# Turned scores of two latent units in four row groups, units of neighbouring head pairs alternating

## The chip, the cores and the metric

One core of a Trainium2 chip runs one program, and the metric is its device time in microseconds, the median of several executions. In what follows PE is TensorE, DVE is VectorE, ACT is ScalarE, POOL is GpSimd and SP is the engine that issues the loads.

## The reference, cut to what matters

The program is a network of ten phases over 512 tokens of width 1024 in fp32: feed-forward layers, a windowed-attention mixer, a state-space mixer, and at the end two layers of a second kind (mixer "mix2", then a feed-forward layer). Only the second kind of mixer is changed. It has a grouped attention of 8 heads and a latent attention of 8 heads; each latent head has 64 plain ("nope") and 32 rotated ("rope", here: turned) score dimensions, and all heads share one turned key:

```python
qb = (rmsnorm(cq, q_a_norm_g) @ w_q_up).reshape(b, s, MLA_HEADS, MLA_QK_DIM)
q_nope, q_rope = qb[..., :MLA_NOPE_DIM], qb[..., MLA_NOPE_DIM:]     # 64 and 32 wide
q_rope = apply_axial_rope(q_rope, cos_b, sin_b)
k_nope, vb = kvb[..., :MLA_NOPE_DIM], kvb[..., MLA_NOPE_DIM:]
k_rope = apply_axial_rope(kr, cos_b, sin_b)                          # one for all heads
qb = jnp.concatenate([q_nope, q_rope], axis=-1)[:, :, :, None, :]
kb = jnp.concatenate([k_nope, k_rope], axis=-1)
yb = blocked_attention(qb, kb, vb, 1.0 / math.sqrt(MLA_QK_DIM))      # softmax(q k^T) v
gates = jax.nn.sigmoid(gl + b_gate)
merged = g_a * (ya @ w_branch_a) + g_b * (yb @ w_branch_b)
return merged @ w_o
```

The score of a latent head is so a sum of two products, one over 64 rows and one over 32 rows.

## The kernel before, in words

**Units.** Attention is worked off in units. A unit is 128 queries (block n of 4) of a pair of heads (the two "sides"), against all 512 keys. A mix2 layer has 32 units: 16 grouped ones (4 head pairs of 4 blocks, `grouped_units`, L1607) and then 16 latent ones (`latent_units`, L1615), pair j = 0 to 3 outside, block n inside. Side 0 of a pair lies in partitions 0 to 63, side 1 in 64 to 127. The turned parts are packed by four heads: head 2j + side lies in the 32 partitions of quarter (2j + side) % 4 of `b_qr[:, j // 2]`, and `b_kr` holds the shared turned key four times, once in each quarter.

**One step of PE** (`attend_pe`, L744). Step s issues in this order, waits included, since every engine works its queue in order:
- the scores of unit s into `scores[g % 2]`, g being the running number of the unit: for a grouped unit one product per side over 64 rows (the pair of sides runs in two row groups); for a latent unit that pair of 64-row products and then a pair of 32-row products on top (L757 to L760). It waits for the exponentials of unit g - 2 (`probs_ready`, L755), which free the buffer;
- the transposes of unit s - 3 (BEHIND = 3, L773), side 0 into bank 5 and side 1 into bank 6, when POOL has scaled it (`probs_scaled`) and the banks have been copied out (`copied_a`, `copied_b`);
- the product with the values of unit s - 4 (L786, "attend"), into bank 4 or 7 (HEADS), which the head pairs use in turn. The first unit of a head pair waits until the pair before the last has been read out (`head_split`, L782).

**The other engines.** DVE (`attend_dve`) takes the row maximum of unit s (L800), scales it (L806, L809), inverts the sums of unit s - 1 (L816), copies side 1 of the turned probabilities of unit s - 3 (L822), and at the end of a head pair forms its low part (L827) one step after ACT formed the high part (L858). ACT (`attend_act`) copies side 0 of unit s - 3 (L838), then does the exponentials of unit s (L850, two sides, each with a read of its sum), then the high part of a head pair that has ended. POOL (`attend_pool`) multiplies the probabilities by the inverted sums (L866). Nothing is loaded that this stretch waits for.

**The end of the attention.** `fill` lists work put ahead of a step: in mix2 two "gate" projections (24 products each, L289 to L291) at steps 34 and 35, each with a wait for all exponentials and for the split of all head pairs but the last (L749, L750). They write the next accumulator bank, tile number % 5 (ACCS), counted through the program. The attention of the first mix2 layer ends at tile 336, that of the second at tile 464, so the first gate writes bank 1 in the first layer and bank 4, which is also one of HEADS, in the second. After the last attend PE waits for the last head pair to be split and begins the branch products (L1798 to L1800).

The step in the code that the change replaces:

```python
many = len(u["q"][0])
for part in range(many):
    for side in range(2):
        mm = pe.matmul(scores[g % 2][:, side, 0:u["keys"]], u["q"][side][part], u["k"][side][part],
                       start=part == 0, stop=part == many - 1)
```

Of the kernel before, what the change touches and what calls it, by code (L numbers as in the profile page):

```python
# [126 lines left out]
def build(nc, t, stop=99):  # L127
    with ExitStack() as ctx:
# [615 lines left out]
        def attend_pe(pe, c, units, turned, fill):  # L744

            n = len(units)
            for s in range(n + BEHIND + 1):
                if s in fill:
                    pe.wait_ge(probs_ready, c.units + n)  # L749
                    pe.wait_ge(head_split, c.heads + n // 4 - 1)  # L750
                    fill[s]()
                if s < n:
                    u, g = units[s], c.units + s
                    if g >= 2:
                        pe.wait_ge(probs_ready, g - 1)  # L755
                    many = len(u["q"][0])
                    for part in range(many):  # L757
                        for side in range(2):
                            mm = pe.matmul(scores[g % 2][:, side, 0:u["keys"]], u["q"][side][part], u["k"][side][part],  # L759
                                           start=part == 0, stop=part == many - 1)  # L760
                    for side in range(2):
                        for at, mask in u["masks"]:
                            mm = pe.matmul(scores[g % 2][:, side, at:at + P], e_ident[:], e_mask[:, mask, :], start=False,
                                           stop=True, skip_group_check=True)
                    mm.then_inc(scores_ready, 1)
                if 0 <= s - BEHIND < n:
                    u, g = units[s - BEHIND], c.units + s - BEHIND
                    pe.wait_ge(probs_scaled, g + 1)
                    for side, (done, free) in enumerate(((turned_a, copied_a), (turned_b, copied_b))):
                        if g:  # L770
                            pe.wait_ge(free, g)
                        for j in range(u["keys"] // P):
                            mm = pe.transpose(bank[TURNED + side][:, j * P:(j + 1) * P],  # L773
                                              pbuf[:, g % 4, side, j * P:(j + 1) * P], ident[:])
                        mm.then_inc(done, 1)
                if 0 <= s - BEHIND - 1 < n:
                    u, g = units[s - BEHIND - 1], c.units + s - BEHIND - 1
                    pe.wait_ge(copied_a, g + 1)
                    pe.wait_ge(copied_b, g + 1)
                    hd = c.heads + (s - BEHIND - 1) // 4  # L780
                    if (s - BEHIND - 1) % 4 == 0 and hd >= 2:
                        pe.wait_ge(head_split, hd - 1)  # L782
# [8 lines left out]
        def attend_dve(dve, ch, c, units, turned):  # L791
            n = len(units)
            for s in range(n + BEHIND + 3):
# [29 lines left out]
                e = s - BEHIND - 2  # L823
                if 0 <= e < n and e % 4 == 3:
                    u, hd = units[e], c.heads + e // 4
                    dve.wait_ge(head_rounded, hd + 1)
                    dve.tensor_tensor(u["lo"], bank[HEADS[hd % 2]][:], u["hi"].bitcast(F32), ALU.subtract)\  # L827
                       .then_inc(head_split, 1)

        def attend_act(act, c, units, turned):  # L830
            n = len(units)
            for s in range(n + BEHIND + 2):
# [21 lines left out]
                e = s - BEHIND - 1  # L854
                if 0 <= e < n and e % 4 == 3:
                    u, g, hd = units[e], c.units + e, c.heads + e // 4
                    act.wait_ge(attended, g + 1)
                    act.activation(u["hi"], bank[HEADS[hd % 2]][:], ACT.Copy).then_inc(head_rounded, 1)  # L858
# [17 lines left out]
        def even_units():  # L876
            units = []
            for j, pair in enumerate(EVEN_PAIRS):
                keys = pair[0] // 3 // 2
                for n in range(NB):  # L880
                    lo, hi = max(n - 1, 0), min(n + 1, NB - 1)
                    halves = (slice(0, HD), slice(HD, P))
                    units.append(dict(
                        q=[[e_qk[half, 2 + j, n * P:(n + 1) * P]] for half in halves],
                        k=[[e_qk[half, keys, lo * P:(hi + 1) * P]] for half in halves],
                        keys=(hi - lo + 1) * P, scale=HD ** -0.5, col=None, n=n, nsink=e_nsink[:, j, :],
# [28 lines left out]
        def even_pe(pe, c, e):  # L915
# [36 lines left out]

            def pooled_part():
                pe.wait_ge(pool_split, 2)
                pe.wait_ge(w_rest, B + OPEN)
# [651 lines left out]
        def grouped_units():  # L1607
            halves = (slice(0, HD), slice(HD, P))
            return [dict(q=[[b_qk[half, j, n * P:(n + 1) * P]] for half in halves], k=[[b_qk[half, 4, :]] for half in halves],
                         keys=S, col=8 * j + 2 * n, n=n, nsink=None, masks=[],  # L1610
# [4 lines left out]
        def latent_units():  # L1615
            halves = (slice(0, HD), slice(HD, P))
            quarters = [slice(32 * i, 32 * i + 32) for i in range(4)]
            return [dict(q=[[b_qn[halves[side], j, n * P:(n + 1) * P],
                             b_qr[quarters[(2 * j + side) % 4], j // 2, n * P:(n + 1) * P]] for side in range(2)],
                         k=[[b_kn[halves[side], j, :], b_kr[quarters[(2 * j + side) % 4], :]] for side in range(2)],  # L1620
                         keys=S, scale=QK ** -0.5, col=None, n=n, nsink=None, masks=[],
                         v=[[b_vb[:, j, m * P + side * HD:m * P + (side + 1) * HD] for m in range(4)] for side in range(2)],
                         hi=yb_hi[:, j, :], lo=yb_lo[:, j, :])
                    for j in range(4) for n in range(4)]

# [53 lines left out]
        def mix2_pe(pe, c, e):  # L1679
# [99 lines left out]
            units = grouped_units() + latent_units()  # L1779

            def gate():
                project(pe, k, k.tiles, [xs_of(xh, xl, KD)])
                k.tiles += 1
            attend_pe(pe, k, units, mix2_turned, {len(units) + BEHIND - 1: gate, len(units) + BEHIND: gate})
            for m in range(KD):
                if m:
                    gate()
                    gate()
                else:
                    pe.wait_ge(head_split, c.heads + len(units) // 4)  # L1790
# [552 lines left out]
```

## Time and profile before

| | |
|---|---|
| median of 3 runs | 3642.07 us (3642.05 to 3642.74) |
| the profiled execution's own time | 3638.86 us |
| its span, first to last instruction | 3637.1 us |
| granted TensorE clock, mean | 0.991 |
| PE busy | 3552.4 us (98%) |
| DVE, ACT, POOL busy | 1432.1, 1342.4, 1899.8 us |
| HBM read | 296.46 MB, 82 GB/s over the span |

The profile is one execution. The span lies within the execution's own time; the difference is what surrounds the program. A busy share is an average over all ten phases. Whether an edit to one phase counts is read from the waits and the order of time in that phase. A matmul in fp32 shows as two records (two passes over the same columns), and two matmuls in different row groups show as records that overlap.

### The profile page before, as it was taken

To read this page: it belongs to the slowest core of one execution; us is meant where nothing else is said; L and a number is where in the kernel's file an instruction comes from. 1 tells how busy PE (TensorE), PEld (TensorE's weight loads), DVE (VectorE), ACT (ScalarE), POOL (GpSimd) and SP (SyncE) were. 2 spreads that over 40 slices of the span, in tenths; PEclk is the share of its full clock that TensorE was granted. 3 is DMA by queue.
4 is the path that set the end of the run, shared out by engine and by line. 5 is a ranking of instruction groups with operands and counts; after the bars stand their busy time and mean duration, and the time that the engine had idled before them with its cause. 6 is when DMAs were issued, how large, how long until landed. Compare 5 with 4: busy or idle time off the path is not lost.

```text
span 3637.1 us, 45438 instructions
## 1 busy us (share of the span) xinstructions
PE 3552.4 (98%) x18086; PEld 2847.0 (78%) x18086; DVE 1432.1 (39%) x2315; ACT 1342.4 (37%) x2172; POOL 1899.8 (52%) x2364
## 2 busy tenths in 40 slices
PE   8999999999999999999999999999999999999998
PEld 7888868888888888548888875778888866878887
DVE  4221765221532158775321355325111564234022
ACT  4232354232422235564332336334232344334231
POOL 6555546555555557525655455545555454546452
PEclk9999999999999999999999999999999999999999
DMA  3333302333232323102333320222333210323332
GB/s 129 96 92 96 104 23 94 96 95 96 92 99 93 94 94 99 38 14 88 99 95 95 108 71 1 64 87 88 99 93 99 91 47 12 93 81 96 96 94 74
DMA packets 87715, 301.50 MB, mean 83 GB/s; under 512 B 9936, under 2 KB 14544, under 8 KB 87120
## 3 DMA queue, kind: packets, MB, share of 16 engines
q1 hardware_dynamic: 85392, 296.50, 26.2%
q8 instruction: 144, 2.36, 0.3%
q10 hardware_dynamic: 2112, 2.10, 0.2%
q14 instruction: 67, 0.55, 0.0%
HBM read 296.46 MB, written 2.10 MB: 82 GB/s over the span
## 4 chain that ended last, share of the span: by engine, by line
PE 91%; DVE 7%; ACT 1%; issue 0%; DMA 0%; SPq 0%; DVEq 0%; ACTq 0%
PE bank L289 25%; PE bank L291 25%; PE bank L290 24%; PE scores L759 3%; PE bank L786 2%; PE bank L773 2%; DVE sqsum L453 1%; DVE xl L443 1%; DVE x L418 1%; DVE tmp L411 1%; PE bank L1798 1%; PE bank L1800 1%; PE bank L1799 1%; PE bank L505 1%; PE bank L506 1%; PE bank L1238 1%
## 5 line engine op out<-in xcount | busy, mean ns | idle before, releaser
L283 POOL TENSOR_TENSOR w_lo<-w_raw,w_hi 128x256 fp32r<-128x256 f32 x2214 | 1681.9, 793 | 1451.6 <-ACT w_hi L271 1451.0
L271 ACT ACTIVATE w_hi<-w_raw 128x1024 fp32r<-128x1024 f32 (+2 forms) x567 | 586.3, 1037 | 1235.4 <-DMA w_raw<-in_ffn_up 374.0
L289 PE MATMUL bank<-xh,w_hi 128*128 128x512 f32 x2544 | 998.1, 392 | 1.2 <-DVE o_g L1449 1.2
L291 PE MATMUL bank<-xh,w_lo 128*128 128x512 f32 x2544 | 990.1, 389 | 0.0
L290 PE MATMUL bank<-xl,w_hi 128*128 128x512 f32 x2544 | 990.0, 389 | 0.0
L289 PEld LDWEIGHTS bank<-xh,w_hi 128*128 128x128 f32 x2544 | 478.4, 188 | 103.7 <-issue 3.1
L290 PEld LDWEIGHTS bank<-xl,w_hi 128*128 128x128 f32 x2544 | 478.5, 188 | 100.0 <-issue 2.4
L291 PEld LDWEIGHTS bank<-xh,w_lo 128*128 128x128 f32 x2544 | 478.4, 188 | 100.0
L289 PE MATMUL bank<-hh,w_hi 128*128 128x512 f32 (+1 forms) x1336 | 501.9, 376 | 0.0
L290 PE MATMUL bank<-hl,w_hi 128*128 128x512 f32 (+1 forms) x1336 | 500.8, 375 | 0.0
L291 PE MATMUL bank<-hh,w_lo 128*128 128x512 f32 (+1 forms) x1336 | 500.8, 375 | 0.0
L290 PEld LDWEIGHTS bank<-hl,w_hi 128*128 128x128 f32 x1336 | 251.2, 188 | 50.0
L289 PEld LDWEIGHTS bank<-hh,w_hi 128*128 128x128 f32 x1336 | 251.1, 188 | 50.0
L291 PEld LDWEIGHTS bank<-hh,w_lo 128*128 128x128 f32 x1336 | 251.1, 188 | 49.9
L866 POOL TENSOR_TENSOR work<-work,red 128x1024 f32<-128x1024 f32 (+2 forms) x88 | 151.3, 1720 | 149.9 <-DVE red L816 149.9
L672 DVE TENSOR_TENSOR work<-bank,sqsum 128x512 f32<-128x512 f32 x88 | 60.7, 690 | 360.9 <-PE bank L291 360.9
L740 DVE COPY y<-bank 128x512 f32<-128x512 f32 x49 | 33.9, 691 | 425.5 <-PE bank L291 425.5
L505 PE MATMUL bank<-xh,w_hi 128*128 128x256 f32 x480 | 124.6, 289 | 19.1 <-ACT xh L475 19.1
L800 DVE TENSOR_REDUCE red<-scores 128x2 f32<-128x1024 f32 (+2 forms) x88 | 98.1, 1115 | 95.0 <-PE scores L759 90.3
L659 ACT ACTIVATE hh<-work 128x512 fp32r<-128x512 f32 x88 | 55.7, 633 | 183.8 <-DVE work L676 183.8
L506 PE MATMUL bank<-xh,w_lo 128*128 128x256 f32 x480 | 122.6, 285 | 0.0
L669 DVE TENSOR_TENSOR work<-bank,sqsum 128x512 f32<-128x512 f32 x88 | 60.8, 691 | 156.5 <-PE bank L291 156.4
(361 smaller groups left out, 4116.5 us busy)
## 6 DMA issues: line engine op xcount, KB each, us to landing
w_raw<-in_ffn_up SPq DMA_DIRECT2D x176, 512.0 KB, 3.5
w_raw<-in_ffn_down SPq DMA_DIRECT2D x64, 512.0 KB, 3.5
w_raw<-in_b_ffn_up SPq DMA_DIRECT2D x64, 512.0 KB, 3.5
w_raw<-in_b_ffn_down SPq DMA_DIRECT2D x64, 512.0 KB, 3.5
w_raw<-in_b_gates SPq DMA_DIRECT2D x48, 512.0 KB, 3.5
w_raw<-in_od_in SPq DMA_DIRECT2D x33, 512.0 KB, 3.3
w_raw<-in_ffn_down SPq DMA_DIRECT2D x32, 384.0 KB, 3.1
w_raw<-in_b_in SPq DMA_DIRECT2D x24, 512.0 KB, 3.3
```

The lines of the kernel that those rows point to most:

```text
L271: act.activation(w_hi[:, g % RING, 0:widths[g]], w_raw[:, g % RING, 0:widths[g]], ACT.Copy)\
L283: ins = pool.tensor_tensor(w_lo[:, slot, part], w_raw[:, slot, part], w_hi[:, slot, part].bitcast(F32), ALU.subtract)
L289: pe.matmul(out, wh, hi, start=first, stop=False)
L290: pe.matmul(out, wh, lo, start=False, stop=False)
L291: return pe.matmul(out, wl, hi, start=False, stop=last)
L505: pe.matmul(out, w_hi[:, slot, k * P:(k + 1) * P], xh[:, k, half(h)], start=k == 0, stop=False)
L506: pe.matmul(out, w_lo[:, slot, k * P:(k + 1) * P], xh[:, k, half(h)], start=False, stop=False)
L759: mm = pe.matmul(scores[g % 2][:, side, 0:u["keys"]], u["q"][side][part], u["k"][side][part], start=part == 0, stop=part == many - 1)
L773: mm = pe.transpose(bank[TURNED + side][:, j * P:(j + 1) * P], pbuf[:, g % 4, side, j * P:(j + 1) * P], ident[:])
L786: mm = pe.matmul(bank[HEADS[hd % 2]][side * HD:(side + 1) * HD, u["n"] * P:(u["n"] + 1) * P], u["v"][side][j], turned[g % 2][:, side, j * ...
L800: ch.link(dve.reduce_max(r[:, 0:2], scores[g % 2][:, :, 0:u["keys"]], mybir.AxisListType.X))
L866: pool.tensor_tensor(p, p, red[:, g % 4, 8:10].unsqueeze(2).broadcast_to([P, 2, u["keys"]]), ALU.mult)\
```

## The change

It does the following.

- Latent units of neighbouring head pairs alternate: (pair 0, block 0), (pair 1, block 0), (pair 0, block 1), and so on, then pairs 2 and 3. The order of all other work on a unit stays.
- The 64-row product of each latent unit stays where it was. The 32-row products of two following units, four matmuls, are issued together ("joint") in the step of the first of them, after that step's transposes and ahead of its attend. They lie in the four quarters of the partitions and write the four banks of both score buffers. The first unit's two add to its 64-row product, the second unit's two open its sum, and its 64-row product is added in the next step.
- Since the joint products write both score buffers, they wait for the exponentials of unit g - 1, not g - 2. The first unit's `scores_ready` is given after the second of the four.
- The running head number comes from the unit (`head`), and so do the ends of the heads (`n == 3`), since two head pairs are now open at once.
- The wait for `head_split` moves out of `attend_pe` into the fills. In mix2 it is taken only where a gate writes bank 4 or 7; where the first gate does (`late`), it is issued at step 35 instead of 34, and the second one behind the last attend.

```diff
--- before.py
+++ after.py
@@ -747,22 +747,20 @@
             for s in range(n + BEHIND + 1):
                 if s in fill:
                     pe.wait_ge(probs_ready, c.units + n)
-                    pe.wait_ge(head_split, c.heads + n // 4 - 1)
                     fill[s]()
                 if s < n:
                     u, g = units[s], c.units + s
                     if g >= 2:
                         pe.wait_ge(probs_ready, g - 1)
-                    many = len(u["q"][0])
-                    for part in range(many):
-                        for side in range(2):
-                            mm = pe.matmul(scores[g % 2][:, side, 0:u["keys"]], u["q"][side][part], u["k"][side][part],
-                                           start=part == 0, stop=part == many - 1)
+                    for side in range(2):
+                        mm = pe.matmul(scores[g % 2][:, side, 0:u["keys"]], u["q"][side], u["k"][side],
+                                       start=u["opens"], stop=u["closes"], skip_group_check=True)
                     for side in range(2):
                         for at, mask in u["masks"]:
                             mm = pe.matmul(scores[g % 2][:, side, at:at + P], e_ident[:], e_mask[:, mask, :], start=False,
                                            stop=True, skip_group_check=True)
-                    mm.then_inc(scores_ready, 1)
+                    if not u["joint"]:
+                        mm.then_inc(scores_ready, 1)
                 if 0 <= s - BEHIND < n:
                     u, g = units[s - BEHIND], c.units + s - BEHIND
                     pe.wait_ge(probs_scaled, g + 1)
@@ -773,12 +771,20 @@
                             mm = pe.transpose(bank[TURNED + side][:, j * P:(j + 1) * P],
                                               pbuf[:, g % 4, side, j * P:(j + 1) * P], ident[:])
                         mm.then_inc(done, 1)
+                if s < n and units[s]["joint"]:
+                    u, g = units[s], c.units + s
+                    pe.wait_ge(probs_ready, g)
+                    for q, (query, key) in enumerate(u["joint"]):
+                        mm = pe.matmul(scores[(g + q // 2) % 2][:, q % 2, 0:u["keys"]], query, key, start=q >= 2, stop=q < 2,
+                                       skip_group_check=True)
+                        if q == 1:
+                            mm.then_inc(scores_ready, 1)
                 if 0 <= s - BEHIND - 1 < n:
                     u, g = units[s - BEHIND - 1], c.units + s - BEHIND - 1
                     pe.wait_ge(copied_a, g + 1)
                     pe.wait_ge(copied_b, g + 1)
-                    hd = c.heads + (s - BEHIND - 1) // 4
-                    if (s - BEHIND - 1) % 4 == 0 and hd >= 2:
+                    hd = c.heads + u["head"]
+                    if u["n"] == 0 and hd >= 2:
                         pe.wait_ge(head_split, hd - 1)
                     many = u["keys"] // P
                     for j in range(many):
@@ -821,8 +827,8 @@
                         dve.wait_ge(attended, g - 1)
                     dve.tensor_copy(turned[g % 2][:, 1, 0:u["keys"]], bank[TURNED + 1][:, 0:u["keys"]]).then_inc(copied_b, 1)
                 e = s - BEHIND - 2
-                if 0 <= e < n and e % 4 == 3:
-                    u, hd = units[e], c.heads + e // 4
+                if 0 <= e < n and units[e]["n"] == 3:
+                    u, hd = units[e], c.heads + units[e]["head"]
                     dve.wait_ge(head_rounded, hd + 1)
                     dve.tensor_tensor(u["lo"], bank[HEADS[hd % 2]][:], u["hi"].bitcast(F32), ALU.subtract)\
                        .then_inc(head_split, 1)
@@ -852,8 +858,8 @@
                                              accum_out=r[:, 4 + side:5 + side])
                     ins.then_inc(probs_ready, 1)
                 e = s - BEHIND - 1
-                if 0 <= e < n and e % 4 == 3:
-                    u, g, hd = units[e], c.units + e, c.heads + e // 4
+                if 0 <= e < n and units[e]["n"] == 3:
+                    u, g, hd = units[e], c.units + e, c.heads + units[e]["head"]
                     act.wait_ge(attended, g + 1)
                     act.activation(u["hi"], bank[HEADS[hd % 2]][:], ACT.Copy).then_inc(head_rounded, 1)
 
@@ -881,8 +887,9 @@
                     lo, hi = max(n - 1, 0), min(n + 1, NB - 1)
                     halves = (slice(0, HD), slice(HD, P))
                     units.append(dict(
-                        q=[[e_qk[half, 2 + j, n * P:(n + 1) * P]] for half in halves],
-                        k=[[e_qk[half, keys, lo * P:(hi + 1) * P]] for half in halves],
+                        q=[e_qk[half, 2 + j, n * P:(n + 1) * P] for half in halves],
+                        k=[e_qk[half, keys, lo * P:(hi + 1) * P] for half in halves],
+                        opens=True, closes=True, joint=None, head=j,
                         keys=(hi - lo + 1) * P, scale=HD ** -0.5, col=None, n=n, nsink=e_nsink[:, j, :],
                         masks=[((m - lo) * P, mask) for m, mask in ((n - 1, 0), (n + 1, 1)) if lo <= m <= hi],
                         v=[[e_v[:, keys, m * P + half.start:m * P + half.stop] for m in range(lo, hi + 1)] for half in halves],
@@ -951,6 +958,7 @@
                             mm.then_inc(blocks_done, 1)
 
             def pooled_part():
+                pe.wait_ge(head_split, c.heads + len(units) // 4 - 1)
                 pe.wait_ge(pool_split, 2)
                 pe.wait_ge(w_rest, B + OPEN)
                 columns_of((0,))
@@ -1606,7 +1614,8 @@
 
         def grouped_units():
             halves = (slice(0, HD), slice(HD, P))
-            return [dict(q=[[b_qk[half, j, n * P:(n + 1) * P]] for half in halves], k=[[b_qk[half, 4, :]] for half in halves],
+            return [dict(q=[b_qk[half, j, n * P:(n + 1) * P] for half in halves], k=[b_qk[half, 4, :] for half in halves],
+                         opens=True, closes=True, joint=None, head=j,
                          keys=S, col=8 * j + 2 * n, n=n, nsink=None, masks=[],
                          v=[[b_va[:, m * P + half.start:m * P + half.stop] for m in range(4)] for half in halves],
                          hi=ya_hi[:, j, :], lo=ya_lo[:, j, :])
@@ -1614,14 +1623,14 @@
 
         def latent_units():
             halves = (slice(0, HD), slice(HD, P))
-            quarters = [slice(32 * i, 32 * i + 32) for i in range(4)]
-            return [dict(q=[[b_qn[halves[side], j, n * P:(n + 1) * P],
-                             b_qr[quarters[(2 * j + side) % 4], j // 2, n * P:(n + 1) * P]] for side in range(2)],
-                         k=[[b_kn[halves[side], j, :], b_kr[quarters[(2 * j + side) % 4], :]] for side in range(2)],
+            rows = [slice(32 * i, 32 * i + 32) for i in range(4)]
+            return [dict(q=[b_qn[half, j, n * P:(n + 1) * P] for half in halves], k=[b_kn[half, j, :] for half in halves],
+                         opens=j % 2 == 0, closes=j % 2 == 1, head=4 + j,
+                         joint=[(b_qr[r, j // 2, n * P:(n + 1) * P], b_kr[r, :]) for r in rows] if j % 2 == 0 else None,
                          keys=S, scale=QK ** -0.5, col=None, n=n, nsink=None, masks=[],
                          v=[[b_vb[:, j, m * P + side * HD:m * P + (side + 1) * HD] for m in range(4)] for side in range(2)],
                          hi=yb_hi[:, j, :], lo=yb_lo[:, j, :])
-                    for j in range(4) for n in range(4)]
+                    for first in (0, 2) for n in range(4) for j in (first, first + 1)]
 
         mix2_turned = [tmp, b_turned]
 
@@ -1778,15 +1787,19 @@
             k.tiles = c.tiles + len(TILES2)
             units = grouped_units() + latent_units()
 
+            late = k.tiles % ACCS in HEADS
+
             def gate():
+                if k.tiles % ACCS in HEADS:
+                    pe.wait_ge(head_split, c.heads + len(units) // 4 - 1)
                 project(pe, k, k.tiles, [xs_of(xh, xl, KD)])
                 k.tiles += 1
-            attend_pe(pe, k, units, mix2_turned, {len(units) + BEHIND - 1: gate, len(units) + BEHIND: gate})
+            attend_pe(pe, k, units, mix2_turned, {len(units) + BEHIND: gate} if late else
+                      {len(units) + BEHIND - 1: gate, len(units) + BEHIND: gate})
             for m in range(KD):
-                if m:
+                for _ in range(2 if m else 1 if late else 0):
                     gate()
-                    gate()
-                else:
+                if m == 0:
                     pe.wait_ge(head_split, c.heads + len(units) // 4)
                 slot = take_block(pe, k)
                 for q, (hi, lo) in enumerate(((ya_hi, ya_lo), (yb_hi, yb_lo))):
```

## Rows read from the trace of the kernel before

**Rows 1.** The page: span, busy time, granted clock by slice, chain that ended last.

```profile
span 3637.1 us, 45438 instructions
...
PE 3552.4 (98%) x18086; PEld 2847.0 (78%) x18086; DVE 1432.1 (39%) x2315; ACT 1342.4 (37%) x2172; POOL 1899.8 (52%) x2364
...
PEclk9999999999999999999999999999999999999999
...
PE 91%; DVE 7%; ACT 1%; issue 0%; DMA 0%; SPq 0%; DVEq 0%; ACTq 0%
```

**Rows 2.** Windows, the two latent stretches: length, busy by engine, granted clock, DMA share.

```profile
2224.72:2291.36 66.64, 66.64 (x515) 36.98 (x513) 35.17 (x69) 34.85 (x85) 30.31 (x17) 1.00 0.00 1
3004.53:3071.17 66.64, 66.64 (x515) 36.98 (x513) 35.16 (x69) 34.86 (x85) 30.32 (x17) 1.00 0.01 1
```

**Rows 3.** Timeline, PE, one latent step: start, length, engine, line, operation, count.

```profile
2253.88 1.13 PE L759 MATMUL scores<-b_kn,b_qn 64*128 64x512 f32 x4
2254.93 1.13 PE L759 MATMUL scores<-b_kr,b_qr 32*128 32x512 f32 x4
2255.99 1.09 PE L773 MATMUL bank<-ident,work 128*128 128x128 f32 x8
2257.02 1.09 PE L786 MATMUL bank<-b_turned,b_vb 128*64 128x128 f32 x16
2258.04 1.13 PE L759 MATMUL scores<-b_kn,b_qn 64*128 64x512 f32 x4
```

**Rows 4.** Timeline, DVE, ACT and POOL, the same latent step.

```profile
2256.11 1.23 DVE L800 TENSOR_REDUCE red<-scores 128x2 f32<-128x1024 f32 x1 [2.08 <-PE scores L759]
2257.37 0.17 DVE L809 TENSOR_SCALAR red<-red 128x2 f32<-128x2 f32 x1
2257.45 0.16 DVE L816 RECIPROCAL red<-red 128x2 f32<-128x2 f32 x1
2257.52 0.67 DVE L822 COPY tmp<-bank 128x512 f32<-128x512 f32 x1
...
2256.69 0.60 ACT L838 ACTIVATE tmp<-bank 128x512 f32<-128x512 f32 x1 [1.83 <-PE bank L773]
2257.57 0.69 ACT L850 ACTIVATE work<-scores,red 128x512 f32<-128x512 f32 x1 [0.29 <-DVE red L809]
...
2258.82 0.20 ACT L850 ACTIVATION_READ_ACCUMULATOR work<-scores,red 128x1 f32 x1
2258.91 0.59 ACT L858 ACTIVATE yb_hi<-bank 128x512 fp32r<-128x512 f32 x1
...
2257.68 1.89 POOL L866 TENSOR_TENSOR work<-work,red 128x1024 f32<-128x1024 f32 x1 [2.27 <-DVE red L816]
```

**Rows 5.** Timeline, PE, narrow windows: single passes of the pairs and the first transposes.

```profile
2254.41 0.60 PE L759 MATMUL scores<-b_kn,b_qn 64*128 64x512 f32 x2
2254.93 0.70 PE L759 MATMUL scores<-b_kr,b_qr 32*128 32x512 f32 x2
...
2177.07 1.02 PE L759 MATMUL scores<-b_qk 64*128 64x512 f32 x4
...
2177.49 1.02 PE L759 MATMUL scores<-b_qk 64*128 64x512 f32 x4
...
2255.99 0.44 PE L773 MATMUL bank<-ident,work 128*128 128x128 f32 x2
```

**Rows 6.** Timeline, the last grouped exponential and the first latent transposes.

```profile
2225.68 0.20 ACT L850 ACTIVATION_READ_ACCUMULATOR work<-scores,red,stat 128x1 f32 x1
...
2226.84 1.09 PE L773 MATMUL bank<-ident,work 128*128 128x128 f32 x8
```

**Rows 7.** Timeline, the last attend of the second layer and what follows it.

```profile
3088.54 1.09 PE L786 MATMUL bank<-b_turned,b_vb 128*64 128x128 f32 x16
...
3090.31 0.69 DVE L827 TENSOR_TENSOR yb_lo<-bank,yb_hi 128x512 fp32r<-128x512 f32 x1 [7.67 <-ACT yb_hi L858]
...
3091.06 0.51 PE L1798 MATMUL bank<-ya_hi,w_hi 128*128 128x512 f32 x1 [1.42 <-DVE yb_lo L827]
```

## The prediction

> **What bounds the kernel now.** I read the page first. PE is busy for 98% of the span, the chain that ended last lies on it for 91%, and the granted clock is full in all slices [rows 1]. That says PE, but an average over ten phases can hide a phase with another limit, so I read the two stretches that the change touches, the sixteen latent units of each mix2 layer, by windows. In both, PE is busy for 66.64 us of 66.64, at clock 1.00, while DVE, ACT and POOL stand at 35, 35 and 30 us and the DMA share is zero [rows 2]. A unit costs 66.64 / 16 = 4.165 us. The timeline of PE within one unit shows what that is: a pair of 64-row products, a pair of 32-row products, the transposes, the attend, and the next unit's scores follow with no gap [rows 3]. From start to start these stages take 1.06 (2253.88 to 2254.93), 1.06, 1.02 and 1.02 us. The 32-row pair fills half as many rows as the 64-row pair and takes as long. So what counts here is the number of stages that PE works through, as long as the others keep up.
>
> **The change, part by part.** About 0.2% (7 us) is what a measurement of this kernel can tell from no change.
>
> *The 32-row products.* Per two units the change removes two 32-row pair stages, 2 x 1.06 = 2.12 us, and adds one stage of four. The trace has no such stage, so its price is bounded. From below: the pair's own 1.06 us, if four run side by side as two do. From above: 2.12 us, if the two pairs follow each other. Serial work of all four, 4.24 us, is further off, and nothing in the trace has 32-row products of different row groups one by one. To choose I take the stage apart. In the layer's first units, where pair follows pair with no change of shape between them, a pass starts 0.43 us after the one before (2177.07 to 2177.49) [rows 5]. Two passes are 0.86, so a pair stage of 1.06 carries 0.20 us beyond them, once as it begins and once as it ends: its first pass takes 0.53 us (2253.88 to 2254.41), its second 0.52 to the next shape [rows 3, 5]. The transposes do nearly the same with one load exposed at their start instead of two: two of them end at 0.44 us and all eight at 1.09, so one is (1.09 - 0.44) / 6 = 0.108, eight are 0.87, and the stage of 1.02 carries 0.15 to 0.16. An exposed weight load of 128 columns is therefore worth about 0.05 us, and four loads instead of two add 0.10. I take 1.16 us for the stage of four: 0.86 of passes, 0.20 of loads, 0.10 of change of shape. It is nearest to the 32-row pair in every respect but the number of loads.
>
> The Trainium skill, page "TensorE: Matmul & The Clock Gate", section on packing small matmuls, has a rule that speaks for less: four 32-row products side by side were measured there at 3.07 times one after another, not four times. With a pair's 1.06 us for one product, that would be 4 x 1.06 / 3.07 = 1.38 us, an estimate by that page, and the sum below would be 11.8 us of gain. No row here shows a stage of four.
>
> Gain: 2.12 - 1.16 = 0.96 us per two units, eight times in a layer, in two layers: 16 x 0.96 = 15.4 us. A layer's two units go from 8.33 to 7.37 us.
>
> *The new wait.* The joint stage waits for the exponentials of unit g - 1. Behind it in PE's queue are the attend of unit g - 4, the next unit's products and everything after; DVE's row maximum waits for it. I put the chain against PE's order, with t the start of the joint stage of an even unit e. PE: joint to 1.16, attend to 2.18, 64-row pair of e + 1 to 3.24, transposes to 4.26, attend to 5.29, 64-row pair to 6.35, transposes to 7.37, next joint. Chain, by the spacings of one unit [rows 4]: DVE starts 0.12 us after the stage's end (2255.99 to 2256.11), ACT's exponentials 1.46 us after that (2257.57), and they take 1.45 us (to 2259.02). For e that is 1.28, 2.74, 4.19. Scores of e + 1 are ready at 3.24; DVE, after the inverse and the copy of 0.67 us, is free at 3.36 and starts; its results would allow the exponentials at 4.82, ACT has copied side 0 (0.60) by 4.79, so they run from 4.82 to 6.27. The next joint is due at 7.37: a slack of 1.1 us, so the wait costs nothing. Where head pairs end, ACT's high part (0.59) and DVE's low part (0.69, rows 7) fall into the chain in different steps, each taking 0.6 or 0.7 of that slack; 0.4 us are left. If this cover went, each 0.1 us of lateness would cost 1.6 us in all.
>
> *Other waits of the new order.* POOL's scaling of e - 1 starts about 2.85 and ends at 4.74 (1.89 us [rows 4]); its transposes come at 6.35. The copy of side 1 of e - 3 ends at 3.36; the transposes that overwrite its bank reach side 1 at about 3.75. This is the tightest place, 0.4 us. The first joint stage comes where the transposes start at 2226.84 today, and the last grouped exponentials end at 2225.88 [rows 6]: no stall. The first unit of a head pair now follows two units after the end of the pair whose bank it takes; its low part is done at about 4.05, its attend due at 4.26. Price if missed: the few tenths by which it is late, some six times in all.
>
> *The end of the attention.* First layer: bank 1, the gates stay where they are; the `head_split` wait that leaves the fill was long satisfied. Second layer: bank 4, so one gate moves behind the last attend. Today PE stands for 1.42 us between the last attend and the first branch product, for the high and low part of the last head pair [rows 7]. After the change the last but one unit ends the pair in bank 4, so the same 1.4 us come ahead of the first gate, and the second gate covers the ones that are there today. Zero in sum. No other queue has a step moved past it: SP and POOL have the same orders, and the loads of the next blocks wait for the same gates in the same order. The even mixer issues what it issued; its `head_split` wait moves within the same fill. Zero.
>
> *Sum.* The profiled execution took 3638.86 us (span 3637.1); less 15.4 that is 3623.5. The median of the runs is 3.2 us above it, so 3642.07 - 15.4 = 3626.7 us.
>
> **The rivals.**
> *The loads of the second passes are not hidden either.* Then both passes of a stage of four pay four loads, 2 x (0.43 + 0.20) + 0.10 = 1.36 us; gain 0.76 x 16 = 12.2, time 3629.9 us. Against it: pair after pair runs at 0.43 us a pass, loads hidden [rows 5]; for it: no row has four loads behind one pass. The page of the Trainium skill named above would land here.
> *The four run only two by two,* by a conflict over four score banks at once or for lack of look-ahead past the first pair. The stage is 2.02 to 2.12 us, the change doesn't do what it says, gain 0 to 1.6 us, time 3641 to 3642 us. For it: the trace never has more than two row groups at work. Against it: the attend's two sides and both pairs start together and show no cost of company.
> *The new wait becomes the bound (slower).* If DVE or ACT took the units strictly one after another, a pair would last twice the chain from scores to exponentials, 2 x 3.03, plus joint and 64-row stage, 1.16 + 1.06, plus one copy ahead of each exponential, 2 x 0.6: 9.5 us against 8.33, so 16 x 1.15 = 18 us slower, 3660 us. It decides once the chain of two units passes 8.33 us; my count gives 6.3 and 1.1 of slack to PE's own 7.37. A chain between 7.4 and 8.3 gives back part of the gain, 3627 to 3641.
>
> **How the numbers follow.** The stage of four at 1.06 to 1.2 us with no stall: 0.66 (3625 to 3627.5). Loads exposed: 0.17. Chain late in part: 0.06. Two by two: 0.07. Slower: 0.04. The range holds the first two and small stalls of up to 0.1 us per two units: low end at the 1.06 bound, 17.0 us of gain, less a microsecond of spread between runs, 3624; high end 3629.9 plus 1.6 and spread, 3632. Faster by over 0.2% are the first two and most of the third, 0.88; within it the two-by-two case and the rest of the third, 0.08; slower 0.04.
>
> **What would show it.** The latent windows should last about 59 us instead of 66.64 with PE busy throughout; the stage of 32-row products should appear once per two units, eight records, with a length from its start to the attend's of 1.16 us; the wait of PE for ACT's exponentials ahead of it should be absent; the stall of 1.4 us in the second layer should stand ahead of the first gate and no longer ahead of L1798. A stage of four over 1.3 us speaks for the first rival, about 2.1 for the second, and PE idle ahead of the joint stage for the third. Unchanged latent windows make the prediction wrong.

## The result, and the profile after

The changed kernel takes 3622.09 us (median of 5, 3619.07 to 3625.31) against 3642.05 for the kernel before (3634.18 to 3642.74): ratio 0.995, interval 0.9938 to 0.9962, 20.0 us less. Five more runs on another occasion, in turns with fifteen of the kernel before, gave 3622.04 against 3638.09: 16.1 us less, ratio 0.9957, interval 0.9944 to 0.9969. The profiled execution took 3619.07 us, its span is 3617.2.

The page after, the lines that answer to [rows 1]:

```profile
span 3617.2 us, 45434 instructions
...
PE 3535.4 (98%) x18086; PEld 2844.0 (79%) x18086; DVE 1433.0 (40%) x2315; ACT 1340.5 (37%) x2172; POOL 1895.6 (52%) x2364
...
PEclk9999999999999999999999999999999999999999
```

The page shows next to nothing: PE was the bound and is the bound (the chain that ended last lies on it for 92%, before for 91%), and no matmul has gone (x18086 in both). The windows of the two latent stretches, cut so that they hold the same 515 records of PE as in [rows 2], show the gain (length, then busy time of PE, its loads, DVE, ACT, POOL, then granted clock, DMA share, GB/s):

```profile
2222.45:2280.77 58.32, 58.32 (x515) 34.73 (x513) 34.92 (x69) 33.87 (x85) 30.34 (x17) 1.00 0.01 1
2992.49:3050.81 58.32, 58.32 (x515) 34.73 (x513) 34.92 (x69) 33.87 (x85) 30.34 (x17) 1.00 0.01 1
```

The same 515 records take 58.32 us instead of 66.64, PE still without a gap. The timeline of PE, beside [rows 3]:

```profile
2237.02 1.13 PE L756 MATMUL scores<-b_kn,b_qn 64*128 64x512 f32 x4
2238.08 1.09 PE L771 MATMUL bank<-ident,work 128*128 128x128 f32 x8
2239.10 1.14 PE L778 MATMUL scores<-b_kr,b_qr 32*128 32x512 f32 x8
2240.17 1.09 PE L792 MATMUL bank<-tmp,b_vb 128*64 128x128 f32 x16
```

Eight records, the four products, lie in one stage of 1.07 us (2239.10 to 2240.17), where four records took 1.06. A window on the beginning of such a stage, one joint stage earlier, shows how: all eight loads start within 0.13 us (the row spans 0.31, one load 0.18), so they lie beside each other, and the first passes of all four products start together (four records of 0.69 span 0.71).

```profile
2231.81 0.31 PEld L778 LDWEIGHTS scores<-b_kr,b_qr 32*128 32x128 f32 x8 [0.17 <-issue]
...
2231.82 0.71 PE L778 MATMUL scores<-b_kr,b_qr 32*128 32x512 f32 x4
```

The chain through ACT, beside [rows 4]. The second unit's exponentials end at 2237.80 + 0.20 = 2238.00, the joint stage begins at 2239.10: 1.10 us of slack.

```profile
2234.45 0.69 ACT L856 ACTIVATE work<-scores,red 128x512 f32<-128x512 f32 x1 [2.37 <-DVE red L815]
...
2236.55 0.69 ACT L856 ACTIVATE work<-scores,red 128x512 f32<-128x512 f32 x1 [0.16 <-DVE red L815]
...
2237.80 0.20 ACT L856 ACTIVATION_READ_ACCUMULATOR work<-scores,red 128x1 f32 x1
```

This stage is the roomiest kind. Of the eight joint stages of a layer three have 1.10 us of slack, the first 0.93, one 0.89 and three only 0.61 or 0.62, the same in both layers. The small ones stand where head pairs end: ahead of the joint stage at 2246.39, for one, ACT stood idle for 0.66 us until DVE, which had formed a low part before, had the row maximum. No joint stage came late.

The end of the second layer, beside [rows 7]. The stall stands ahead of the first gate (L289), and the branch product follows the second gate at once:

```profile
3055.89 1.09 PE L792 MATMUL bank<-tmp,b_vb 128*64 128x128 f32 x16
3057.03 0.60 ACT L864 ACTIVATE yb_hi<-bank 128x512 fp32r<-128x512 f32 x1 [0.87 <-PE bank L792]
3057.66 0.69 DVE L833 TENSOR_TENSOR yb_lo<-bank,yb_hi 128x512 fp32r<-128x512 f32 x1 [0.97 <-ACT yb_hi L864]
...
3058.45 0.47 PE L289 MATMUL bank<-xh,w_hi 128*128 128x512 f32 x1 [1.47 <-issue]
...
3070.45 0.39 PE L291 MATMUL bank<-xh,w_lo 128*128 128x512 f32 x1
3070.68 0.40 PE L1811 MATMUL bank<-ya_hi,w_hi 128*128 128x512 f32 x1
```

The profile puts this wait down to "issue". That it is the wait for the split is not shown by a releaser; it is read from its place, right behind yb_lo, and from the code.

### The profile page after: what moved, and what is told of

It is laid out like the page before. It is cut to its first block, busy times and chain, and to the rows that moved or that the text cites. A ratio compares the mean times of both kernels' runs of the same rounds, so it can differ in the third digit from the quotient of the medians.

```text
span 3617.2 us, 45434 instructions
## 1 busy us (share of the span) xinstructions
PE 3535.4 (98%) x18086; PEld 2844.0 (79%) x18086; DVE 1433.0 (40%) x2315; ACT 1340.5 (37%) x2172; POOL 1895.6 (52%) x2364
## 4 chain that ended last, share of the span: by engine, by line
PE 92%; DVE 6%; ACT 1%; issue 0%; DMA 0%; SPq 0%; DVEq 0%; ACTq 0%
PE bank L289 25%; PE bank L290 25%; PE bank L291 25%; PE scores L756 2%; PE bank L792 2%; PE bank L771 2%; DVE sqsum L453 1%; DVE xl L443 1%; DVE x L418 1%; DVE tmp L411 1%; PE bank L1811 1%; PE bank L1813 1%; PE bank L1812 1%; PE bank L505 1%; PE bank L506 1%; PE bank L513 1%
## 5 line engine op out<-in xcount | busy, mean ns | idle before, releaser
L289 PE MATMUL bank<-xh,w_hi 128*128 128x512 f32 x2544 | 998.1, 392 | 2.7 <-issue 1.5
L289 PEld LDWEIGHTS bank<-xh,w_hi 128*128 128x128 f32 x2544 | 478.7, 188 | 105.4 <-issue 4.6
L289 PE MATMUL bank<-hh,w_hi 128*128 128x512 f32 (+1 forms) x1336 | 501.9, 376 | 0.0
L289 PEld LDWEIGHTS bank<-hh,w_hi 128*128 128x128 f32 x1336 | 251.1, 188 | 50.2
```

Of the source, the lines that this page charges most:

```text
L289: pe.matmul(out, wh, hi, start=first, stop=False)
```

## The experiments

Theory: the gain is the stage saved, 8 x (2.12 - 1.07) = 8.4 us in each layer, and nothing else; the new wait and the moved gate cost nothing. Rivals: the order gives or costs something of its own; ACT's total work decides and not the place of the wait. One table for all runs, worked out from their timelines: where the first latent product starts in the first layer; the stretch from there to the transposes behind the last 64-row pair; to the first branch product; PE's idle time in the stretch and behind it (each pair of figures is first and second layer). The four kernels with pieces and count_groups were run once each (3621.62, 3626.18, 3624.85, 3630.20 and 3626.27 us, in the order act_pieces8, early_pieces8, act_pieces16, early_pieces16, count_groups); ten runs of the changed kernel lie between 3618.7 and 3626.0, so single times cannot tell them apart by a few us, and their traces are what counts.

| kernel | starts at | stretch | to branch | idle in | idle behind |
|---|---|---|---|---|---|
| before | 2224.72 | 64.58, 64.58 | 86.50, 86.53 | 0, 0 | 1.42, 1.42 |
| changed | 2222.45 | 56.23, 56.23 | 78.12, 78.19 | 0, 0 | 1.42, 1.47 |
| after_again | 2220.61 | 56.23, 56.23 | 78.17, 78.20 | 0, 0 | 1.42, 1.47 |
| alternate_only | 2226.45 | 64.58, 64.58 | 86.47, 86.55 | 0, 0 | 1.42, 1.47 |
| count_groups | 2228.21 | 56.15, 56.15 | 78.09, 78.12 | 0, 0 | 1.42, 1.47 |
| joint_early | 2225.85 | 56.37, 56.38 | 78.31, 78.35 | 0.07, 0.08 | 1.42, 1.47 |
| gates_after | 2229.09 | 56.23, 56.23 | 76.38, 76.92 | 0, 0 | 0, 0.48 |
| act_pieces8 | 2223.96 | 56.23, 56.23 | 78.27, 78.31 | 0, 0 | 1.48, 1.52 |
| early_pieces8 | 2226.82 | 56.38, 56.39 | 78.28, 78.36 | 0.08, 0.08 | 1.42, 1.47 |
| act_pieces16 | 2223.33 | 56.29, 56.29 | 79.33, 79.68 | 0, 0 | 2.44, 2.75 |
| early_pieces16 | 2224.99 | 59.44, 59.44 | 82.36, 82.69 | 2.72, 2.72 | 2.34, 2.66 |

**The changed kernel once more** (no edit).

> The changed kernel once more, in turns with the kernel before on one chip. In the two profiles on hand the latent stretches account for 16.7 us (16 times 2 x 1.06 - 1.07), and some 3 us of the 19.9 us between the spans arose in the state-space mixer, where the granted clock differed (0.77 before, 0.96 after, 1530 to 1545 us). Theory: only the 16.7 us belong to the change. It expects a difference of the medians of 15.5 to 18 us, ratio 0.9954. Rival: the change also moves what comes before and after the latent stretches, difference 19 to 21 us, ratio 0.9945.

Measured: 16.1 us, as the theory has it, and the stretches as in the first trace of the changed kernel. The two stretches give 8.35 us each. The interval of this comparison, 11 to 20 us, would still allow the lower part of the rival's 19 to 21. Two things speak against the rival. All 30 runs of the kernel before have a median of 3639.1 us, the ten of the changed kernel 3622.1, which is 17.0 apart. And in the traces the span without the two parts from the first latent product to the first branch product is 3464.0 us in the kernel before, while over the ten other traces it goes from 3460.5 to 3469.3: the rest of the kernel before takes no longer than that of the others.

What lies ahead of the latent stretches is the same program but for one satisfied wait, and yet the first latent product starts anywhere from 2220.6 to 2229.1 us. A part of it can be placed by the granted clock of the state-space mixer (columns as above, the clock being third from the end), here for the kernel before and the changed one:

```profile
1530.00:1545.00 15.00, 15.00 (x74) 5.45 (x72) 6.65 (x9) 8.16 (x18) 3.86 (x4) 0.77 0.00 1
```

```profile
1530.00:1545.00 15.00, 15.00 (x87) 5.79 (x86) 8.96 (x13) 9.37 (x20) 4.34 (x4) 0.96 0.00 1
```

PE is busy throughout in both, and does 74 instructions at clock 0.77 and 87 at 0.96. In this pair of profiles the changed kernel comes out 2.8 us ahead between 1518 and 1560 us. In another pair it goes the other way: gates_after has 0.93 from 1600 to 1720 us where the changed kernel has 0.97, and loses 3 us there.

**The order alone.** Each latent unit issues its own 32-row pair, and the joint block is gone; units still alternate, gates as in the changed kernel.

```diff
+                    for side, (query, key) in enumerate(u["own"]):
+                        mm = pe.matmul(scores[g % 2][:, side, 0:u["keys"]], query, key, start=False, stop=True,
+                                       skip_group_check=True)
...
-                    if not u["joint"]:
-                        mm.then_inc(scores_ready, 1)
+                    mm.then_inc(scores_ready, 1)
...
-                if s < n and units[s]["joint"]:
...
```

> The units of neighbouring head pairs alternate and the gates stand as in the changed kernel, but each latent unit issues its own pair of 32-row products right behind its 64-row pair, as before. Theory (all of the gain is the stage saved): time as before, within 1.5 us, latent unit 4.165 us. Rival (the order itself gives or costs something through head_split and the moved gate): a difference from before of 2 us or more.

Measured 3639.19 against 3638.09, ratio 1.0003 (0.9994 to 1.0013), stretches of 64.58 us. The medians alone would leave room for up to 4.7 us more. The traces settle it: from the first latent product to the branch products it takes 86.47 and 86.55 us, before 86.50 and 86.53. The order by itself is worth nothing, nor is the moved gate: the stall of 1.47 us only changes its place.

**Row groups counted.**

```diff
-                         joint=[(b_qr[r, j // 2, n * P:(n + 1) * P], b_kr[r, :]) for r in rows] if j % 2 == 0 else None,
+                         joint=[(b_qr[r, j // 2, n * P:(n + 1) * P], b_kr[r, :]) for r in rows[0:n + 1]] if j % 2 == 0 else None,
...
```

> Part of the computation is left out: the joint stage has one 32-row product in block 0, two in block 1, three in block 2, all four in block 3. This measures the stage by the number of row groups. Theory of the prediction (each exposed load costs 0.05 us): 1.01, 1.06, 1.11, 1.16 us, the last of which the changed kernel already contradicts with 1.07. Rival (loads of different row groups run side by side, a row group more costs only the few ns by which it starts later): 1.05, 1.06, 1.065, 1.07 us from the stage's start to the attend's.

The four joint stages of the first two head pairs, each followed by the attend:

```profile
2230.29 1.12 PE L778 MATMUL scores<-b_kr,b_qr 32*128 32x512 f32 x2
2231.34 1.09 PE L792 MATMUL bank<-tmp,b_va 128*64 128x128 f32 x16
...
2237.56 1.13 PE L778 MATMUL scores<-b_kr,b_qr 32*128 32x512 f32 x4
2238.62 1.09 PE L792 MATMUL bank<-tmp,b_va 128*64 128x128 f32 x16
...
2244.83 1.13 PE L778 MATMUL scores<-b_kr,b_qr 32*128 32x512 f32 x6
2245.89 1.09 PE L792 MATMUL bank<-tmp,b_vb 128*64 128x128 f32 x16
...
2252.11 1.14 PE L778 MATMUL scores<-b_kr,b_qr 32*128 32x512 f32 x8
2253.18 1.09 PE L792 MATMUL bank<-tmp,b_vb 128*64 128x128 f32 x16
```

From joint start to attend start: 1.05, 1.06, 1.06, 1.07 us for one, two, three and four row groups. My price of 0.05 us per load is refuted: three row groups more, with six loads more, cost 0.02 us together. This kernel leaves out 24 of the 64 products over 32 rows, so it measures a stage and is no version of the program.

Four products side by side come to 4 x 1.05 / 1.07 = 3.9 times four stages that each hold one product and stand between stages of another shape. No run has four such products directly one after another. By the 0.43 us from pass to pass without a change of shape [rows 5] they would take 8 x 0.43 + 0.20 = 3.6 us, an estimate, and four side by side would be 3.4 times as fast. The Trainium skill, page "TensorE: Matmul & The Clock Gate", section on packing small matmuls, measured 3.07. Both figures of this case lie above it, and the stage of 1.07 us, not the 1.38 that this factor gave, is what decides here. The span model of the Trainium skill in the same section, one product plus some 4 ns for each further one, agrees in kind: 0.02 us for three more.

**The joint stage ahead of the transposes** (the block moved up by one stage).

> The joint stage moves ahead of the step's transposes, so the second unit's scores come one stage of 1.02 us later behind it while the next joint is due after the same 7.29 us. My chain count gives 1.1 us of slack with the joint stage where the change has it; here 0.1 us would be left, and less than none where a head pair ends. Theory: latent stretches 0 to 2 us longer in each layer than in the changed kernel, with PE idle on ACT's exponentials ahead of some joint stages. Rival (the chain has much more slack than I counted): no idle time at all, the same time as the changed kernel.

Measured: 3622.53 us, ratio 0.9955, stretches 0.14 and 0.15 us longer than in the changed kernel, of which 0.07 or 0.08 is idle time.

```profile
2255.91 0.20 ACT L856 ACTIVATION_READ_ACCUMULATOR work<-scores,red 128x1 f32 x1
...
2256.19 1.14 PE L768 MATMUL scores<-b_kr,b_qr 32*128 32x512 f32 x8
```

The exponentials end at 2256.11 and the joint stage begins at 2256.19, so the slack is the 0.1 us that the count gave. It is 0.08 at seven of the eight joint stages of a layer. At the first one the joint stage begins 0.05 us behind the exponentials, the least that these traces show between the two, and there the idle time lies. That the ends of head pairs would break it was wrong. ACT's high part of 0.60 us falls where ACT would otherwise wait for the transposes, 0.78 us in this variant, and no joint stage behind DVE's low part is late either.

**ACT made slower.** Its copy of side 0 is cut into pieces, once with the joint stage where the change has it and once ahead of the transposes.

```diff
-                    act.activation(turned[g % 2][:, 0, 0:u["keys"]], bank[TURNED][:, 0:u["keys"]], ACT.Copy)\
-                       .then_inc(copied_a, 1)
+                    latent = u["nsink"] is None and u["col"] is None
+                    cuts = [round(q * u["keys"] / 8) for q in range(9)] if latent else [0, u["keys"]]
+                    for a, b in zip(cuts, cuts[1:]):
+                        ins = act.activation(turned[g % 2][:, 0, a:b], bank[TURNED][:, a:b], ACT.Copy)
+                    ins.then_inc(copied_a, 1)
```

> ACT's copy of side 0 of a latent unit is made in 8 pieces of 64 columns, which lengthens it from 0.57 us to an estimated 1.6, worked out from the 0.57 us of the whole copy and the 0.09 us after which a read of one column lets the next instruction start. The joint stage stays where the change has it. Theory (a slack of 1.10 us ahead of the joint stage, as the trace of the changed kernel shows): the longer copy takes about 1.0 of it, so no idle time except where a head pair ends, 0 to 1.5 us per layer. Rival (ACT's throughput is already the bound near): 4 us or more per layer.

> The same copy in 8 pieces, and the joint stage ahead of the transposes, where the trace of that variant shows 0.08 us of slack. ACT has the same work as in the run before. Theory (the wait for the exponentials is a chain that the joint stage's place can bring to the path): each joint stage comes 0.4 to 0.8 us late, 3 to 6.5 us more per layer than the changed kernel, with PE idle on ACT's exponentials. Rival (only ACT's total work counts): the same time as the run before.

Within the stretch neither shows more idle time than without the pieces. The next instruction starts only 0.104 us later for each piece (from 2237.30 to 2238.13 for eight). With the joint stage early, the exponentials waited 0.29 us for DVE behind the whole copy (joint_early, copy at 2253.78, exponentials at 2254.67); the longer copy falls into that wait, and they start as long after its beginning as before (2240.18 to 2241.06). So the load was too small to tell the theories apart: inconclusive. With 16 pieces (16 and range(17) in the edit):

> The copy in 8 pieces took 0.83 us from its start to the next instruction, 0.104 us a piece, not the 1.6 I had estimated, so it took too little of the slack to test anything. With 16 pieces of 32 columns it should take 1.66 us, 1.1 us more than the whole copy. The joint stage stays where the change has it. Theory (slack of 1.10 us): it is used up to the last tenth, so PE is idle 0 to 0.15 us per joint stage and up to 0.6 where a head pair ends, 0 to 2.5 us per layer. Rival (ACT's total work decides; per two units it is 2 x (1.45 + 1.66) = 6.2 us of 7.29): no idle time in either of these two runs.

> The same copy in 16 pieces with the joint stage ahead of the transposes. Theory (a chain that the place of the joint stage can bring to the path): in that variant the copy starts when its transposes are done, and the exponentials behind it would begin 0.7 to 0.9 us later than without the pieces, with 0.08 us of slack; so each joint stage comes 0.6 to 0.8 us late, 4.5 to 7 us more per layer than the changed kernel. Rival (ACT's total work decides): no more than the run before.

From the first of sixteen pieces to the next instruction's start it took 1.22 and 1.25 us in the two kernels, not the 1.66 expected. With the joint stage in the change's place PE has no idle time within the stretch. Its joint stages keep 0.47 us of slack or more, but for one in each layer, where a head pair ends: there the load is released by the exponentials, and the stage begins 0.06 us late.

```profile
2269.18 0.31 PEld L778 LDWEIGHTS scores<-b_kr,b_qr 32*128 32x128 f32 x8 [0.23 <-ACT work L859]
```

With the same work on ACT and the joint stage earlier PE does wait for them, as PE's waits of that kernel (2222 to 2290 us; total, times, longest) show:

```profile
PE scores L768 <- ACT work L859: 2.6, 6, 0.5
```

Six joint stages of the layer come late, five by 0.42 us and one by 0.55, and the layer's stretch is 3.2 us longer than in the changed kernel, below the 4.5 to 7 expected since the copy was shorter. So the new wait is real and would reach the path if it came one stage earlier under a slower ACT; where the change puts it, its cover is 1.10 us at most and 0.61 at least. The rival, ACT's total, is out: that is equal in the two runs (busy 1368.2 and 1369.1 us). The pieces cost 1.0 and 1.3 us behind the stretch, where the last transposes wait 0.7 and 0.4 us for the copies (first layer); this was not expected.

**Both gates behind the last attend.**

```diff
-            attend_pe(pe, k, units, mix2_turned, {len(units) + BEHIND: gate} if late else
-                      {len(units) + BEHIND - 1: gate, len(units) + BEHIND: gate})
+            attend_pe(pe, k, units, mix2_turned, {})
...
-                for _ in range(2 if m else 1 if late else 0):
+                for _ in range(2):
```

> Both gate projections of each layer stand behind the last attend, none in the fill. In the changed kernel PE is idle for 1.42 us in the first layer (ahead of the first branch product) and for about as long in the second (ahead of the first gate). Theory: with two gates between the last attend and the branch products the first layer's stall is covered, and in the second the last attend (1.02 us) covers all but 0.4 us of the read-out of the pair in bank 4: 1.4 + 1.0 = 2.4 us less than the changed kernel, from the first latent product to the first branch product 76.7 and 77.1 us instead of 78.1 and 78.2. Rival: the transposes of the last unit now wait for POOL's scaling, which the first gate used to hide, and the gain is under 1 us. In the medians 2.4 us is about the noise, so the traces decide.

The stretch to the branch is 76.38 and 76.92 us, 1.7 and 1.3 less than in the changed kernel, with 0.48 us of idle time left in the second layer; 0.2 to 0.3 us more than expected. A change of shape between gate and attention falls away too, which would be worth about 0.2 by the rows of the changed kernel (0.34 us instead of 0.23 from the first product of the second gate to the next, 3065.11 to 3065.45, and 0.32 instead of 0.23 from the last product of the first gate to the attend, 3063.77 to 3064.09); no run tests that. The time, 3624.01 against 3640.28 (ratio 0.9955, 0.9941 to 0.9968), can't tell 3 us from nothing: its latent part began 6.6 us later than in the profile of the changed kernel. By the traces of this stretch it is the best version; by the times of the runs that is not shown.

## Why the prediction was right or wrong

**Right:** PE as the bound of the stretch, one stage saved per two units, no stall at the joint wait (slack counted 1.1, found 1.10 us; where head pairs end, 0.4 were said to be left, and 0.61 were), no stall at the transition, zero in sum at the end of the second layer, and faster.

**Wrong, the size of a term.** The step "an exposed weight load of 128 columns is therefore worth about 0.05 us, and four loads instead of two add 0.10" failed. It compared two stages of different shape, the transposes and a pair, and took the difference for one load more; and it counted loads one after another that the trace shows beside each other, all eight starting within 0.13 us. The stage of four measured 1.07 us, not 1.16, at the lower bound that the prediction had set (1.06). The gain is 16 x (2.12 - 1.07) = 16.8 us by that sum and 16.7 by the stretches, not 15.4. By this term alone the forecast would have been 3625.3 us.

**Wrong, the range.** The time of 3622.09 us lies 4.6 below the forecast of 3626.7: 1.3 by the stretches is the term above, and 3.3 is not the change. With the right price for the stage alone the forecast would still have been missed by 3.2 us. The step that failed is the low end of the range: "17.0 us of gain, less a microsecond of spread between runs, 3624". That microsecond rested on three runs within 0.7 us of each other. The kernel before has since run from 3634.0 to 3644.4 us, and the changed one from 3618.7 to 3626.0. The forecast started from 3642.07, and the median of all 30 runs of the kernel before is 3639.1; less 16.7 that is 3622.4. In other words, the gain of 15.4 us lies within both measured intervals, and the base it was taken from was about 3 us high by the luck of the draw.

A part of that spread was placed in the state-space mixer's clock. The prediction had read from the page that the granted clock "is full in all slices", but a digit 9 there stands for 90% or more of a slice of 91 us, and in 15 us of that same trace the clock was 0.77. For the latent stretches the reading held (1.00), for the spread it hid what mattered. Why the clock differs from run to run stays open.

The rivals: the loads exposed in both passes, four products two by two, and the joint wait as the bound were all out by the first trace.

## What to carry to other kernels

On a path that is bound by TensorE, count stages rather than rows: products over 32 rows in different row groups, writing different banks, cost four what one costs (1.07 us against 1.05 here), so it pays to reorder neighbouring units until four can be issued together. Before putting a wait into such a queue, count the chain behind it against the queue's own order; the count from one unit's timeline gave the slack of a plain step to a hundredth of a microsecond, since the wrong price of the stage stands on both sides of it and falls out. Take the smallest slack and not the usual one: here 0.61 us instead of 1.10, where a head pair ends. And where a change is worth half a per cent, take the spread from runs in turns on one occasion, and the size from the stretch that changed.

## What the runs showed of the hardware

The length of a stage of fp32 products over 32 rows and 512 columns hardly depends on how many row groups it fills: 1.05, 1.06, 1.06 and 1.07 us for one to four at granted clock 1.00, with eight loads of 0.18 us starting within 0.13 us.

Short copies on ACT in a row overlap, and leave something behind. The next instruction starts 0.104 us after a copy of 64 columns and 0.077 after one of 32, where the record of one of 512 columns lasts 0.59 to 0.60. But each record ends a little later than this spacing, 0.113 and 0.088 us behind the one before, and what has piled up shows in the instructions behind: the exponentials' record, 0.69 us otherwise, lasts 0.76 after eight pieces and 0.85 after sixteen (act_pieces8, act_pieces16). So in the early variant with sixteen pieces the exponentials start 0.36 us later after the copy's beginning than without pieces (1.25 against 0.89) and take 0.17 us longer to end (1.61 against 1.44); together, less the slack of 0.08, that is 0.45, near the 0.42 us by which the joint stages were late.
